# A two-layer hybrid encoder on one core: reciprocal roots in joint chains, and three pieces of work in other places

## The reference, cut to what matters

```python
for l in range(2):
    h = rms_norm(x, norm_mix[l])
    q_a, k_a, v_a, u_b, q_c, k_c, v_c, g_c = split(h @ w_in[l])       # 1024 x 2048
    y_a = window_attention(rms_norm(q_a), rms_norm(k_a), v_a, sinks[l])  # 8 heads of 64, 2 of keys
    y_b = multiscale_pool(u_b)                                        # 256 wide
    y_c = silu(g_c) * rms_norm(retention(rope(q_c), rope(k_c), v_c))  # 4 heads of 64
    x = x + concat(y_a, y_b, y_c) @ w_out[l]
    h2 = rms_norm(x, norm_ffn[l])
    # 32 experts in 8 groups; a token goes to the two best of its best group
    x = x + sum(gate_w * (silu(h2 @ w_gate) * (h2 @ w_up)) @ w_down)
```

## Time and profile before

| | us |
|---|---|
| median of three runs | 3119.68 |
| lowest, highest | 3116.94, 3121.95 |
| the profiled execution, its own time | 3100.88 |
| its span in the trace | 3099.0 |

### The profile page before, as it was taken

How to read it: one execution, slowest core, us unless ns; L and a number is a source line. 1 busy time by engine, 2 the same in 40 slices (tenths; PEclk the granted TensorE clock), 3 DMA queues, 4 the chain that set the end, 5 groups by cost and what they waited for, 6 DMA issues and landing times.

```text
span 3099.0 us, 55779 instructions
## 1 busy us (share of the span) xinstructions
PE 3045.9 (98%) x18148; PEld 2173.3 (70%) x18148; DVE 1477.8 (48%) x4514; ACT 618.1 (20%) x1922; POOL 1048.6 (34%) x1250
## 2 busy tenths in 40 slices
PE   8999999999899999999999999999998999999998
PEld 4455555554699999888755555555557999998887
DVE  5577777767422222211156777777773222221111
ACT  1222222222111111101123223223231111111101
POOL 1132132133255555423212232222332555563322
PEclk9999999999999999999999999999999999999999
DMA  8756656653789999999865557566537899999996
GB/s 306 264 182 245 222 192 249 219 190 111 269 282 306 315 317 352 342 357 345 322 245 192 190 220 252 182 230 244 189 121 256 286 306 306 327 352 346 346 355 214
DMA packets 248192, 817.18 MB, mean 264 GB/s; under 512 B 68016, under 2 KB 121264, under 8 KB 188720
## 3 DMA queue, kind: packets, MB, share of 16 engines
q1 hardware_dynamic: 201200, 735.20, 64.1%
q0 software_dynamic: 46112, 77.70, 10.8%
q10 hardware_dynamic: 576, 0.52, 0.1%
HBM read 718.87 MB, written 95.56 MB: 263 GB/s over the span
## 4 chain that ended last, share of the span: by engine, by line
PE 88%; DVE 4%; DMA 3%; issue 2%; DVEq 1%; ACT 1%; SPq 1%; POOL 0%; ACTq 0%; POOLq 0%
PE bank L2033 31%; PE bank L1734 17%; PE bank L1799 13%; PE bank L2073 9%; PE bank L2063 6%; PE bank L1705 5%; PE bank L1659 2%; PE bank L1926 1%; PE bank L1960 1%; PE bank L1885 1%; DMA out<-arena 1%; DMA arena<-in_x 1%; DMA wts<-wt 1%; PE bank L1810 0%; DMA arena<-hrows,arena 0%
## 5 line engine op out<-in xcount | busy, mean ns | idle before, releaser
L2033 PEld LDWEIGHTS bank<-arena,wts 128*128 128x128 f32 x8192 | 987.1, 191 | 22.2 <-issue 22.2
L2033 PE MATMUL bank<-arena,wts 128*128 128x128 f32 (+7 forms) x8192 | 991.2, 283 | 7.9 <-DVE arena L1613 7.1
L1734 PE MATMUL bank<-wts 128*128 128x512 f32 x1056 | 471.0, 598 | 1.7 <-DMA wts<-wt 1.5
L1799 PE MATMUL bank<-wts,arena 128*128 128x512 f32 x1024 | 456.2, 598 | 1.6 <-ACT arena L1048 1.6
L1636 DVE TENSOR_TENSOR arena<-arena,bank 128x128 f32<-128x128 f32 (+6 forms) x64 | 19.1, 299 | 902.7 <-ACT arena L1110 902.7
L1734 PEld LDWEIGHTS bank<-wts 128*128 128x128 f32 x1056 | 194.3, 190 | 223.8 <-issue 216.1
L826 POOL DMA_INDIRECT arena<-hrows,arena x288 | 292.2, 1015 | 167.7 <-issue 152.0
L1799 PEld LDWEIGHTS bank<-wts,arena 128*128 128x128 f32 x1024 | 189.2, 190 | 215.4 <-issue 212.7
L722 POOL TENSOR_TENSOR arena<-arena 128x256 f32<-128x256 f32 x32 | 23.1, 722 | 814.4 <-DVEq L1389 814.4
L851 POOL DMA_INDIRECT out<-arena x176 | 275.1, 1563 | 53.8 <-issue 51.2
L2073 PE MATMUL bank<-arena,wts 128*128 128x135 f32 (+6 forms) x2176 | 280.0, 289 | 0.0
(11 more groups left out here) (262 smaller groups left out, 3172.8 us busy)
## 6 DMA issues: line engine op xcount, KB each, us to landing
wts<-in_w_gate SPq DMA_DIRECT2D x128, 1024.0 KB, 8.7
wts<-in_w_up SPq DMA_DIRECT2D x128, 1024.0 KB, 11.0
wts<-in_w_down SPq DMA_DIRECT2D x128, 1024.0 KB, 17.1
wts<-wt SPq DMA_DIRECT2D x96, 1024.0 KB, 6.7
wts<-in_w_in SPq DMA_DIRECT2D x88, 1024.0 KB, 9.0
hrows<-arena SPq DMA_DIRECT2D x36, 512.0 KB, 7.6
out<-arena SPq DMA_DIRECT2D x36, 512.0 KB, 4.1
wt<-arena SPq DMA_DIRECT2D x16, 1024.0 KB, 4.1
```

What stands on the lines that cost most here:

```text
L1734: i = mm(bIP[j in (1, 3, 6)][:, :], own[:, d], ring[k % SLOTS][:, d], start=(d == 0 and j in (0, 1, 3)), stop=(d == 3), skip_group_check=True)
L1799: i = mm(bIP[k][:, :], dT[o][:, d - 4] if d in (4, 5) else mixT[:, d], wout[:, d, 512 * k:512 * k + 512], start=(n == 0), stop=(n == DC - 1))
L2033: return mm(gu_at(f, k, w), lhs, xT[:, d, 0:w], start=start, stop=(d == DC - 1), skip_group_check=True)
```

## The change

Five edits, in the order of the program:

1. **First tile by halves.** DVE scales and turns the first tile of a layer in two halves of 128 columns per quarter; PE starts on the first (`first_half`) and waits for `hT_ready` at its fifth chunk. In the first layer, ACT's queue issues the loads of `par` and of the tile's rows (0.9 MB together) instead of SP's.
2. **Joined chains.** `rstd` takes several sources. In steps 2 to 13 the root of the rows after mixing (`norm_2` of the step before) is the eleventh column of the chain for queries and keys; `h2n` is made behind it. In steps 1 to 12 the root of input tile s + 3 joins that of the retention's output.
3. **The fold of the squares moves.** For that, ACT's `sumsq_front(s + 3)` stands behind the exponentials, and PE's `sumsq(s + 3)` behind the router's parts.
4. **Late steps.** In steps 14 and 15 (`LATE`) the root of queries and keys comes behind the probabilities, and `qk_scaled` behind `z_ready`. `norm_2` stays as it was from step 13 on.
5. **Second expert.** Each of its six gathers has a semaphore of its own, and `second_in` waits, turns and scales group by group.

The diff, cut:

```diff
-GATHERS = (0,) + GROUPS[1:]
+GATHERS = (0, 0) + GROUPS[2:]
...
+LATE = TILES - 2
...
-        xss, rfq = part("mix", 4), part("mix", 4)
+        xss, zrf = part("mix", 4), part("mix", 8)
+        zr, rfq = zrf[:, 0:4], zrf[:, 4:8]
...
                     load_pieces(0, range(2))
-                    load_par()
-                    load_x(xr[0], xr_full[0], 0)
...
-                        for g in range(GATHERS[i]):
+                        for g in range(GROUPS[i]):
                             e.indirect_dma_start(xg[b][:, g * PIECE:(g + 1) * PIECE], None, hpieces, bass.IndirectOffsetOnAxis(
-                                ap=piece[:, i, g:g + 1].bitcast(U32), axis=0)).then_inc(gathered[b], 16)
+                                ap=piece[:, i, g:g + 1].bitcast(U32), axis=0)).then_inc(second_rows[g] if i == 1 else gathered[b], 16)
...
                 with e.If(l == 0):
                     first_pieces(x)
+                    e.dma_start(par[:, :], small[0:1].rearrange("o p n -> p (o n)")).then_inc(par_full, 16)
+                    e.dma_start(xr[0], x[0:P, :]).then_inc(xr_full[0], 16)
...
                         a(stat[:, 40:48], stat[:, 32:40], ACT.Exp).then_inc(exp_done, 1)
+                        if s + 3 < TILES:
+                            sumsq_front(s + 3)
                     if s == 1:
...
-                        a(squares, xr[o], ACT.Square, accum_out=stat[:, 4:5]).then_inc(sumsq_2, 1)
+                        at = 62 if s + 1 < LATE else 4
+                        a(squares, xr[o], ACT.Square, accum_out=stat[:, at:at + 1]).then_inc(sumsq_2, 1)
...
                         e.drain().then_inc(pT_ready, 1)
-                        if s + 3 < TILES:
-                            sumsq_front(s + 3)
...
-            def rstd(dst, src, n):
+            def rstd(dst, *sums):
 
                 w = dst.shape[1]
                 val, y, t, half = newton[:, 0:w], newton[:, 16:16 + w], newton[:, 32:32 + w], newton[:, 15:16]
-                v.tensor_scalar(val, src, 1.0 / n, EPS, ALU.mult, ALU.add)
+                at = 0
+                for src, n in sums:
+                    v.tensor_scalar(newton[:, at:at + src.shape[1]], src, 1.0 / n, EPS, ALU.mult, ALU.add)
+                    at += src.shape[1]
...
                 def norm_of(t):
 
-                    e.wait_ge(pe_sumsq, l * (TILES - 1) + t)
-                    rstd(rfq, bB[:, 256:260], D)
+                    if t < 4:
+                        e.wait_ge(pe_sumsq, l * (TILES - 1) + t)
+                        rstd(rfq, (bB[:, 256:260], D))
...
-                    rstd(stat[:, 52:62], stat[:, 52:62], HD)
+                    if s >= LATE:
+                        return
+                    if s < 2:
+                        rstd(stat[:, 52:62], (stat[:, 52:62], HD))
+                        return
+                    e.wait_ge(sumsq_2, l * TILES + s - 1)
+                    rstd(stat[:, 52:63], (stat[:, 52:62], HD), (stat[:, 62:63], D))
+                    v.tensor_scalar(stat[:, 1:2], stat[:, 62:63], -1.0, None, ALU.mult).then_inc(r2_ready, 1)
+                    h2n_of(s - 1, stat[:, 62:63])
...
-                def norm_2(s, o):
-
-                    t0 = l * TILES + s
-                    e.wait_ge(sumsq_2, t0)
-                    rstd(stat[:, 5:6], stat[:, 4:5], D)
-                    v.tensor_scalar(stat[:, 1:2], stat[:, 5:6], -1.0, None, ALU.mult).then_inc(r2_ready, 1)
-                    if s == TILES:
-                        return
-                    if isinstance(s, int) and s == 1:
+                def h2n_of(s, factor):
+
+                    if s == 1:
                         e.wait_ge(pad_rows, PAD_STORES * 16)
                     else:
-                        e.wait_ge(h_stored, (t0 - 1) * 16)
-                    v.tensor_scalar(h2n, xr[o], stat[:, 5:6], None, ALU.mult).then_inc(h2n_ready, 1)
+                        e.wait_ge(h_stored, (l * TILES + s - 1) * 16)
+                    v.tensor_scalar(h2n, xr[(s - 1) % 2], factor, None, ALU.mult).then_inc(h2n_ready, 1)
+
+                def norm_2(s):
+
+                    e.wait_ge(sumsq_2, l * TILES + s)
+                    rstd(stat[:, 5:6], (stat[:, 4:5], D))
+                    v.tensor_scalar(stat[:, 1:2], stat[:, 5:6], -1.0, None, ALU.mult).then_inc(r2_ready, 1)
+                    if s < TILES:
+                        h2n_of(s, stat[:, 5:6])
...
                     if s == 0:
                         e.wait_ge(xq_full, (l * TILES + 1) * 64)
-                        v.tensor_tensor(xq.rearrange("p (g c) -> p g c", g=4), xq.rearrange("p (g c) -> p g c", g=4),
-                                        bc(gmix.unsqueeze(1), [P, 4, PIECE]), ALU.mult)
-                        e.drain()
-                        turn_of(0)
+                        for k in range(2):
+                            half = xq.rearrange("p (g c) -> p g c", g=4)[:, :, P * k:P * k + P]
+                            v.tensor_tensor(half, half, bc(gmix[:, P * k:P * k + P].unsqueeze(1), [P, 4, P]), ALU.mult)
+                            e.drain()
+                            v.transpose(whole_hT(0).rearrange("p (d g n) -> p g d n", d=DC, g=4)[:, :, 4 * k:4 * k + 4],
+                                        xq.rearrange("p (g d n) -> p g d n", g=4, d=DC)[:, :, 4 * k:4 * k + 4])
+                            e.drain().then_inc(hT_ready if k else first_half, 1)
...
-                    if front and back:
+                    if front and back and s < LATE:
                         qk_scaled(s)
+                    elif front and back:
+                        rstd(stat[:, 52:62], (stat[:, 52:62], HD))
...
-                        rstd(stat[:, 48:52], stat[:, 48:52], HD)
+                        if s + 3 < TILES:
+                            e.wait_ge(pe_sumsq, l * (TILES - 1) + s + 3)
+                            rstd(zrf, (stat[:, 48:52], HD), (bB[:, 256:260], D))
+                        else:
+                            rstd(zr, (stat[:, 48:52], HD))
                         for k in range(2):
                             v.tensor_tensor(z[:, k], (bE, bF)[k][:, 256:384].rearrange("p (h e) -> p h e", h=2),
-                                            bc(stat[:, 48 + 2 * k:50 + 2 * k].unsqueeze(2), [P, 2, HD]), ALU.mult)
+                                            bc(zr[:, 2 * k:2 * k + 2].unsqueeze(2), [P, 2, HD]), ALU.mult)
                         e.drain().then_inc(z_ready, 1)
+                    if front and s >= LATE:
+                        qk_scaled(s)
...
                         if s % 2 and s < 12:
                             add_blocks(s)
-                        norm_2(s, o)
+                        if s + 1 >= LATE:
+                            norm_2(s)
...
+                    e.drain()
...
+                    def second_in():
+
+                        step = WIDTHS[1] // GROUPS[1]
+                        xT = xT_at(1, WIDTHS[1])
+                        for g in range(GROUPS[1]):
+                            e.wait_ge(second_rows[g], turn * 16 + 16)
+                            v.transpose(windows(xT_all[1], g * step, DC, 32 * GMAX, 32), xg[1][:, g * PIECE:(g + 1) * PIECE])
+                            e.drain()
+                            own = xT[:, :, g * step:g * step + step]
+                            v.tensor_tensor(own, own, bc(gffn8.unsqueeze(2), [P, DC, step]), ALU.mult)
+                        e.drain().then_inc(xT_ready, 1)
+                        e.nop().then_inc(x_turned, 1)
...
-                        if i < NE - 1:
+                        if i == 0:
+                            second_in()
+                        elif i < NE - 1:
                             x_in(i + 1, n + 1, 1 - b, WIDTHS[i + 1])
...
                         if part[0] == 0:
-                            if t < WHOLE and n == 0:
+                            if t == 0 and n == 0:
+                                e.wait_ge(first_half, l + 1)
+                            elif t < WHOLE and n == 0:
                                 e.wait_ge(hT_ready, l * TILES + t + 1)
...
+                            if t == 0 and n == 0 and d == 4:
+                                e.wait_ge(hT_ready, l * TILES + 1)
...
-                        if back:
-                            e.wait_ge(kvd_read, t0)
+                        if back and s > 1:
+                            e.wait_ge(kvd_read, t0 - 1)
...
@@ -1909,10 +1960,10 @@
                     fill(4)
                     if tail and s != TILES:
                         router_parts()
+                    if back and s + 3 < TILES:
+                        sumsq(s + 3)
                     if back:
                         rv = rows_of(s - 1)[:, RV0:RV0 + RW]
-                        if s + 2 < TILES:
-                            e.wait_ge(hT_ready, t0 + 3)
...
                     fill(7)
-                    if back and s + 3 < TILES:
-                        sumsq(s + 3)
```

8 lines of the change are left out of this document (5 added, 3 removed).

## The result

| | before | changed kernel |
|---|---|---|
| median, us | 3119.16 (4 runs, 3116.94 to 3121.95) | 3099.34 (4 runs, 3096.86 to 3099.97) |
| ratio to before | | 0.9931, 95% interval 0.9916 to 0.9946 |
| profiled execution, us | 3100.88 | 3099.97 |
| its span | 3099.0 | 3098.1 |

The change takes 19.8 us off the median (by the centre of the ratio 21.5); forecast were 23.2, with 3096.5 for the time and 3087 to 3107 as the range. But the two profiled executions differ by only 0.9 us. So the first thing to see is that the recorded execution of before, on which the whole sum was built, was not one like the others: those took 18.8 us more. The changed kernel's was like its others. One execution of the whole study, of e4 (3197.99 us), had a lower granted clock, 0.946, and is left out.

The account below looks back on a forecast made before the run. PE, busy 98% of the span, was taken as the bound, with at most 53 us of idle time to end. Gains of 7.4 + 4.6 + 10.9 + 0.3 = 23.2 us from 3119.7 gave 3096.5 us, range 3087 to 3107.

Parts of the forecast that it names:

- The fold: Middle steps on PE: moved behind the router's parts, the fold costs 0.06 us instead of 0.38; gain 7.4 us.
- The joint chains: Middle steps: some 5 us of DVE a step go, but PE does not wait there; gain 0, at most 1 us.
- The late steps: Steps 14 and 15, both layers: z_ready comes 1.2 us earlier a step; gain 4.6 us, range 2 to 6.
- The second expert: Rows ready 0.2 us before PE comes: 7.1 us of waits and 3.8 of slow clock go; gain 10.9 us.
- the prediction's own sign: Second expert's row: the prediction would be wrong if a wait above 1 us stayed there.
- rival (b): Second expert still waits: half the wait and all the clock loss stay, gain 3.5 us, 3103.9 us; chance .08.
- The first tile: Second layer's first product: half the tile is ready sooner, 0.3 us gained; first layer 0.
- rival c: Loads at the start fall otherwise: up to 6.2 us more gain (3090.3) or 3 us loss (3099.5); chance .08.
- From the profiled execution to the median: Median before lay 18.8 us above the profiled execution; that difference was taken to carry over to the changed kernel.
- (a): Middle steps: the fold costs 0.38 us at its new place too; gain 15.8 us, 3103.9 us; chance .15.
- (d): Middle steps: PE waits for ACT's squares at the fold every step, so slower, about 3128 us; chance .03.
- (e): Late steps give nothing, z_ready comes no earlier; 3101 us; chance .04.

Follow-up runs that it names:

- e4: Kernel before with only steps 14 and 15 changed: root of queries and keys behind the probabilities, scaling behind z; 3113.16 us, ratio 0.9981.
- e3: Kernel before with only the fold of the squares moved (ACT's squares behind the exponentials, PE's fold behind the router's parts); 3117.88 us, ratio 0.9997.
- e1: Kernel before, unchanged, run again for a second trace; median 3119.52 us against 3118.84, ratio 1.0001.
- e2: Kernel before with only the second expert's rows turned and scaled group by group; 3118.63 us, ratio 0.9998.
- e8: Kernel before with half the gate and up weights loaded in the second layer, and the second expert's rows group by group; 3113.01 us, ratio 0.9984.
- e9: Changed kernel without the first tile by halves, its moved loads and the second expert's group-wise rows; 3101.00 us, ratio 0.9941 to the kernel before.
- e5: Kernel before with only the first joint chain: norm_2's root as eleventh column of the queries and keys chain; 3116.20 us, ratio 0.9994.
- e6: Kernel before with the fold moved and both joint chains, nothing else; 3105.02 us, ratio 0.9960.
- e7: Kernel before with only half of each expert's gate and up weights loaded in the second layer; 3113.20 us, ratio 0.9984.
- e10: Changed kernel without PE's branch over the first expert of a second round; 3095.30 us, ratio 0.9925 to the kernel before.

## Why the prediction was right, and where it was wrong

The time fell inside the range, 2.8 us above the forecast. That it came so near is luck: of the steps behind it two held and two missed, 10.9 us too many at the second expert and some 6 too few at the joint chains.

- **The fold (7.4 forecast).** The size was right: 0.38 us at the old place, 0.04 at the new (0.06 was taken), 0.33 off each step. The rule that the prediction cites from the Trainium skill, on a drain at a change of the tiling mode, agrees with 0.38 and 0.04; no run separates it from other reasons. The cover for ACT's squares held too: no wait behind them. But the fold alone brought nothing (e3). The step that failed is the sentence that none of PE's waits stands in the middle steps. The list of before that the prediction read had one there (L1734, a block product):

```profile
PE bank L1734 <- DMA wts<-wt: 1.5, 2, 1.1
```

And the waits for `x_new` are mostly too short for the list, but recur each step; with the fold moved their sum was as large as the gain.
- **The joint chains (0 forecast, up to 1).** This is the term that was missed. With the fold they are worth 13.5 us by the medians. Of these some 7.5 are the fold's floor (511.45 - 508.05 = 3.4 over the eleven distances, and 0.33 in the first step, in each layer), which the fold alone couldn't bring in, and 6 the waits that were above it (8.5 in the trace of e1). I had named the cover, "PE has work through the middle steps", and `x_new` as what could be late next, and had not measured how thin the cover was: the starts of successive steps in the earlier trace rows lay 46.1 us apart, but other steps had 46.8. And SP's queue was named only for its store; the loads that PE needs stand in it behind the wait for the turned tile.
- **The late steps (4.6 forecast).** 3.1 us by the trace of e4, 5.7 (interval 3 to 9) by the medians. The mechanism was right, the wait behind the probabilities passed to ACT as said; `z` came sooner by less.
- **The second expert (10.9 forecast).** Nothing, in e2 and e8, and nothing that e9 can tell. By the prediction's own sign, a wait above 1 us at the second expert's row, this step was wrong: 1.31 us stood there. Three things were wrong in it. The trace of before showed 3.6 us of wait and a slow clock, and in the other traces without edit 5 the wait is 1.5 to 2.0. Of their second experts only two ran for a part at the lower level of the clock, those of the second layer in e5 and e6, behind 1.93 us each (19.99 us instead of 18.32; granted 0.65 and 0.57 over the first 4 us); e1 had 2.04 us there and a clock of 1.00. Behind the wait stood PE's branch, whose 6.36 us were in the trace of before all along, and I looked for what was late next on DVE and DMA alone. And rival (b), that half of the wait stays, came nearest, but for another reason, and it still had 3.5 us too many.
- **The first tile (0.3 forecast).** The wait ahead of the second layer's first product, 0.24 us in the trace of before and 0 to 0.8 in the others without edit 1, is 0 in the four traces with it. The medians can't show it. The 4.5 us wait stood, as said (rival c fell).
- **From the profiled execution to the median.** The 18.8 us were carried over as a constant. They were not: 12.6 of the 19.5 between the two traces of the kernel before lie in the experts, where PE's sequencer fell short, and 6.6 in the mixing stages, among them the late blocks that the joint chains then took away. So part of what the change saved wasn't in the trace that the sum was built on.

Rivals (a), (d) and (e) fell: 0.04 and not 0.38; no wait for squares; `z` is sooner.

## What to carry to other kernels

Before building a sum on one profiled execution, hold its time against the other runs'. Where it lies 0.6% from them, something worked otherwise in it, and the terms read from it need a second trace. Two edits on two engines that pace each other (PE's fold, DVE's chains) can be worth nothing or little alone and 13 us together: read the distances from step to step, not the list of waits, to see how near the second engine is. Behind a wait that is removed, look at the waiting engine's own sequencer too, its branches first. And a gap at the place of a wait isn't yet a wait: look when the awaited thing landed before you call it late. That a lighter load removes the gap doesn't show it either, since the load touches more than the one transfer.

## What the runs showed of the hardware

A far jump of PE's sequencer took 5.8 to 6.7 us in 36 of 38 cases in the fourteen traces. The branch over the first expert of a second round took 6.1 to 6.4 in 22 of 24 cases; with the light weights of e7 and e8 in the second layer it took 5.0 and 5.6. The jump back at the end of the layers' loop took as long, and the same instruction 0.09 us where it fell through at the end (trace of before):

```profile
L1667 PEldq COMPARE_BRANCH  x2: 86/3164/6243, 1541.7 to 3085.1; - x2
```

PE's queued products hid most of the branch between the experts, and 0.8 to 1.6 us showed where edit 5 had the rows ready. The Trainium skill (Runtime: NRT & Kernel Launch, Instruction fetch mechanics) says that a taken branch to a place outside the loaded pages forces a fetch of the target page; it gives no figure. The traces agree: in the changed kernel two fetches of instructions, 16 KB each, begin at 831.25 and 834.50, the first inside the branch, and in e10, which has no branch there, none of 16 KB begins between 818.69 and 840.50. In 36 of the 38 far jumps of these traces such a fetch begins 3.4 to 4.1 us behind the jump's start and takes 1.0 to 1.1 us, and the jump ends 1.4 to 1.5 us behind it; in the two light cases the fetch begins sooner, at 2.0 and 2.6 us, and the jump is shorter. The Trainium skill (Advanced Engine Details and Errata, Control Flow Timing) has about 108 ns for a compare-and-branch; that is near the 0.09 us of the one that falls through, and where the jump is far the measurement decides, with some 60 times as much.

The same program, with nearly the same bytes (60.6 MB) in packets of weights of the same 0.25 us each, took 183.1 us from the tenth to the eighteenth expert in one execution and 189.0 in another, at 331 and 321 GB/s: the two stages of the experts differed by 12.6 us of 3119 between them. None of the weights came late by their semaphores, and halving those that are loaded took most of the gaps away.
